# Product-key experts on one core: token innermost in the one-hots, bf16 operands in their comparisons and products

## What is computed

```python
q = (xf @ wq).reshape(T, 8, 2, 128)
s = jnp.einsum('thcd,ckd->thck', q, subkeys)
sv, si = lax.top_k(s, 16)                      # per head, per half
cand = (sv[:, :, 0, :, None] + sv[:, :, 1, None, :]).reshape(T, 8, 256)
cv, ci = lax.top_k(cand, 16)
ea = take_along_axis(si[:, :, 0], ci // 16);  eb = take_along_axis(si[:, :, 1], ci % 16)
experts = ea * 128 + eb                        # 128 experts for each token, of 16384
gate = softmax(cv)
act = gelu(einsum('cd,ced->ce', x, u_tab[experts]))
y = einsum('ce,ced->cd', act * gate, v_tab[experts])
```

## Time and profile before

| | |
|---|---|
| time, median of 3 runs | 4366.12 us (4361.21 to 4377.41) |
| the profiled execution's own time | 4377.61 us |
| its span | 4375.8 us |
| TensorE busy | 3942.4 us, 90% |
| VectorE busy | 2018.1 us, 46% |
| ScalarE, GpSimd busy | 895.2 us and 154.4 us |
| first layer's experts, first build to last chunk | 420.7 to 1262 us |
| second layer's experts, first build on | from 1670 us |

### The profile page before, as it was taken

The page is one execution under the profiler, slowest core; times in us unless marked ns, Lnnn a source line. Parts: engine busy times, 40 slices in busy tenths (PEclk is TensorE's granted clock), DMA queues, the critical chain, the costliest instruction groups (busy, mean ns, idle before and its releaser), DMA issues.

```text
span 4375.8 us, 54878 instructions
## 1 busy us (share of the span) xinstructions
PE 3942.4 (90%) x23468; PEld 2746.5 (63%) x23468; DVE 2018.1 (46%) x3441; ACT 895.2 (20%) x1502; POOL 154.4 (4%) x135
## 2 busy tenths in 40 slices
PE   6989999998988899999998979998869999999986
PEld 5778878886777688887876756565643333332333
DVE  4276645748754497255758533355532111111112
ACT  2311111223434111212233421223300000000000
POOL 0000000000000000000000000021200000000000
PEclk9799999999998899999999989999979999999998
DMA  4433323443344333333443331211129999999993
GB/s 182 155 135 138 132 116 131 159 155 135 135 165 155 134 137 125 124 136 135 154 154 123 137 127 49 106 58 58 58 81 413 427 428 427 428 427 428 425 398 145
DMA packets 62282, 846.18 MB, mean 193 GB/s; under 512 B 6800, under 2 KB 8976, under 8 KB 10160
## 3 DMA queue, kind: packets, MB, share of 16 engines
q1 hardware_dynamic: 62032, 842.60, 47.9%
HBM read 841.52 MB, written 1.05 MB: 193 GB/s over the span
## 4 chain that ended last, share of the span: by engine, by line
PE 67%; DVE 15%; DMA 13%; ACT 3%; issue 2%; SPq 0%; POOL 0%; DVEq 0%; ACTq 0%
PE bank L83 65%; DVE arena L119 6%; DMA ring<-in_w_gu_dram 6%; DMA ring<-in_peer_u_dram 3%; DMA arena<-in_w_gu_dram 3%; ACT arena L109 2%; DVE vlo L119 2%; PE bank L96 2%; DVE arena L187 1%; DVE arena L181 1%; DVE arena L193 1%; DVE arena L145 1%; DVE arena L133 1%; DVE arena L125 1%; DVE arena L127 1%
## 5 line engine op out<-in xcount | busy, mean ns | idle before, releaser
L83 PE MATMUL bank<-xT,ring 128*128 128x256 f32 x5120 | 1174.1, 389 | 55.7 <-DMA ring<-in_peer_u_dram 33.4
L83 PEld LDWEIGHTS bank<-xT,ring 128*128 128x128 f32 x5120 | 988.2, 195 | 197.8 <-DMA ring<-in_peer_u_dram 35.9
L83 PE MATMUL bank<-arena 128*128 128x32 bf16 (+7 forms) x9660 | 926.6, 291 | 145.7 <-DVE arena L119 108.5
L83 PEld LDWEIGHTS bank<-arena 128*128 128x128 bf16 (+4 forms) x9660 | 544.4, 126 | 522.9 <-issue 294.5
L83 PE MATMUL bank<-ring,arena 128*64 128x512 f32 (+1 forms) x2304 | 592.5, 606 | 39.5 <-DMA ring<-in_w_gu_dram 33.7
L109 ACT ACTIVATE arena<-bank 128x256 f32<-128x256 f32 (+2 forms) x484 | 223.8, 462 | 1975.2 <-PE bank L83 1484.6
L83 PEld LDWEIGHTS bank<-ring,arena 128*64 128x64 f32 (+1 forms) x2304 | 194.4, 146 | 427.3 <-issue 328.5
L119 DVE TENSOR_TENSOR arena<-arena 128x512 bf16<-128x512 bf16 (+6 forms) x636 | 424.4, 703 | 82.0 <-ACT arena L109 67.9
L119 DVE TENSOR_TENSOR vlo<-ring,vhi 128x1024 fp32r<-128x1024 f32 x256 | 313.2, 1224 | 267.2 <-PE bank L83 249.8
L83 PE MATMUL bank<-vhi,phi 128*128 128x512 f32 x1024 | 432.3, 422 | 0.0
L83 PE MATMUL bank<-vhi,plo 128*128 128x512 f32 x1024 | 406.7, 397 | 0.0
(11 more groups left out here) (105 smaller groups left out, 1665.9 us busy)
## 6 DMA issues: line engine op xcount, KB each, us to landing
ring<-in_w_gu_dram SPq DMA_DIRECT2D x85, 2048.0 KB, 19.3
ring<-in_peer_u_dram SPq DMA_DIRECT2D x64, 2048.0 KB, 8.7
ring<-in_peer_v_dram SPq DMA_DIRECT2D x64, 2048.0 KB, 8.6
arena<-in_w_gu_dram SPq DMA_DIRECT2D x55, 2048.0 KB, 19.4
ring<-in_w_dn_dram SPq DMA_DIRECT2D x41, 2048.0 KB, 17.9
arena<-in_w_dn_dram SPq DMA_DIRECT2D x29, 2048.0 KB, 20.6
ring<-in_w_hg_dram SPq DMA_DIRECT2D x14, 2048.0 KB, 8.6
ring<-in_w_mod_dram SPq DMA_DIRECT2D x12, 2048.0 KB, 7.8
```

The source lines that it names most:

```text
L83: i = self.e.matmul(o, l, r, start=start, stop=stop)
```

## The change

- `Aoh`, `Boh` and `eqb` keep their sizes, but the token becomes the innermost index: `(a t)` and `(b t)` in place of `(t a)` and `(t b)`.
- A new bf16 tensor `keys16` holds every key number repeated for 16 tokens (2048 values). GpSimd writes it at the start of each layer's experts and marks "keys listed"; VectorE waits for that mark ahead of the first hots.
- A new bf16 tensor `e16` holds a and b in bf16 (one conversion of 512 values a layer). The three gate parts are read from `gsb` in bf16, and the last part is written there directly.
- So the comparison and the products have three bf16 operands each, and the innermost index is the token, of step 1 in all of them. The value that is repeated is now repeated along the middle index.
- `pe_build` takes, for token i, the stationary operand `ah[:, :, i]` and the moving operand `bh[:, k, :, i]`: the 128 and the 32 columns now lie 16 elements (32 bytes) apart, where they were adjacent before.
- `eg` and `gs` move into the memory of the routing, which begins lower, and `ROUTED` becomes 45: five more chunks of stage 1 wait for "gates split".

```diff
-ROUTED = 50
+ROUTED = 45
...
+        e16 = ar(256).bitcast(BF16).rearrange("p (c n) -> p c n", c=2)
+        keys16 = ar(1024).bitcast(BF16).rearrange("p (a t) -> p a t", t=16)
...
-        Aoh = [ar(1024).bitcast(BF16).rearrange("p (t a) -> p t a", t=16) for _ in range(2)]
-        Boh = [ar(768).bitcast(BF16).rearrange("p (k t b) -> p k t b", k=3, t=16) for _ in range(2)]
-        eqb = [ar(256).bitcast(BF16).rearrange("p (t b) -> p t b", t=16) for _ in range(2)]
-        top[0] = ARENA - 11200
+        Aoh = [ar(1024).bitcast(BF16).rearrange("p (a t) -> p a t", t=16) for _ in range(2)]
+        Boh = [ar(768).bitcast(BF16).rearrange("p (k b t) -> p k b t", k=3, t=16) for _ in range(2)]
+        eqb = [ar(256).bitcast(BF16).rearrange("p (b t) -> p b t", t=16) for _ in range(2)]
+        top[0] = ARENA - 12736
...
             for i in range(16):
-                P.mm(bG[n % 2][:, i * 32:i * 32 + 32], [(ah[:, i, :], bh[:, k, i, :]) for k in range(3)])
+                P.mm(bG[n % 2][:, i * 32:i * 32 + 32], [(ah[:, :, i], bh[:, k, :, i]) for k in range(3)])
...
-            V.tt(Aoh[n % 2], bc(iota, 1, 16), bc(eg[:, 0, t0:t0 + 16], 2, 128), EQ, lag=FREE)
+            V.tt(Aoh[n % 2], keys16, bc(e16[:, 0, t0:t0 + 16], 1, 128), EQ, lag=0 if n < 2 else FREE)
...
-            V.tt(eqb[n % 2], bc(iota[:, q * 32:q * 32 + 32], 1, 16), bc(eg[:, 1, t0:t0 + 16], 2, 32), EQ, lag=FREE)
+            V.tt(eqb[n % 2], keys16[:, 32 * q:32 * q + 32, :], bc(e16[:, 1, t0:t0 + 16], 1, 32), EQ, lag=FREE)
...
-                V.tt(Boh[n % 2][:, k, :, :], eqb[n % 2], bc(gs[:, k, t0:t0 + 16], 2, 32), MUL, lag=k)
+                V.tt(Boh[n % 2][:, k, :, :], eqb[n % 2], bc(gsb[:, k, t0:t0 + 16], 1, 32), MUL, lag=k)
...
             V.cp(gsb[:, 0, :], eg[:, 2, :])
-            V.cp(gs[:, 0, :], gsb[:, 0, :])
+            V.cp(e16, eg[:, 0:2, :], lag=1)
+            V.cp(gs[:, 0, :], gsb[:, 0, :], lag=1)
...
-            V.tt(gs[:, 2, :], eg[:, 2, :], gs[:, 1, :], SUB)
+            V.tt(gsb[:, 2, :], eg[:, 2, :], gs[:, 1, :], SUB)
             V.mark("gates split", l)
+            V.wait_ge(*at["keys listed", l])
...
         def pool_peer(l):
             after_stage(G, "mix", l)
+            G.cp(keys16, bc(iota, 2, 16))
+            G.mark("keys listed", l)
```

More of the change, by code:

```diff
@@ L905, in build @@
         top[0] = 0
-        eg = ar4(3, 2, 128).rearrange("p k t n -> p k (t n)")
-        gs = ar4(3, 1, 256).rearrange("p k o n -> p k (o n)")
         gsb = ar(384).bitcast(BF16).rearrange("p (k n) -> p k n", k=3)
+        e16 = ar(256).bitcast(BF16).rearrange("p (c n) -> p c n", c=2)
+        keys16 = ar(1024).bitcast(BF16).rearrange("p (a t) -> p a t", t=16)
         H0 = top[0]
@@ L913, in build @@
         v_lo = [vlo_t[:, i * 1024:i * 1024 + 1024] for i in range(2)]
-        Aoh = [ar(1024).bitcast(BF16).rearrange("p (t a) -> p t a", t=16) for _ in range(2)]
-        Boh = [ar(768).bitcast(BF16).rearrange("p (k t b) -> p k t b", k=3, t=16) for _ in range(2)]
-        eqb = [ar(256).bitcast(BF16).rearrange("p (t b) -> p t b", t=16) for _ in range(2)]
-        top[0] = ARENA - 11200
+        Aoh = [ar(1024).bitcast(BF16).rearrange("p (a t) -> p a t", t=16) for _ in range(2)]
+        Boh = [ar(768).bitcast(BF16).rearrange("p (k b t) -> p k b t", k=3, t=16) for _ in range(2)]
+        eqb = [ar(256).bitcast(BF16).rearrange("p (b t) -> p b t", t=16) for _ in range(2)]
+        top[0] = ARENA - 12736
         assert H0 + 256 * ROUTED <= top[0]
+        eg = ar4(3, 2, 128).rearrange("p k t n -> p k (t n)")
+        gs = ar4(3, 1, 256).rearrange("p k o n -> p k (o n)")
         pq = [ar3(4, 256) for _ in range(2)]
```

## The result

The changed kernel takes 4592.19 us (median of 4 runs, 4588.51 to 4596.13) against 4368.38 us before: the ratio is 1.0511, 95% interval 1.0489 to 1.0533. That is 224 us more, where 38 to 40 were forecast. It lies inside the stated range and on the forecast side, but far outside the forecast's own range of 4385 to 4500.

A forecast was written before the change was run, and what follows sets the result against it. TensorE was taken as the bound, VectorE only in places. Per layer +13.1, +25.6 and −18.5 us made +20.2, so +40 for both layers on 4366: 4406 us; range 4258 to 4765, the forecast's own 4385 to 4500.

The forecast's parts named there:

- VectorE's rounds: VectorE's comparison and products per round: two bf16 values at a time, shortening a round by 2.12 us, from 5.33 to 3.21.
- stretch 3: Last window of a layer's experts, 165.3 us, 38 chunks of stage 2 and 16 builds; forecast 146.8 us, −18.5.
- The price of spread columns: TensorE's builds: a matmul with its load rises from 25 to 54 ns, a build by 1.39 us.
- a lost fast load: Rival, TensorE's builds: weight loads fall to float32 speed, 111 ns a matmul, +191 us a layer, 4747 us; chance 0.16.
- one column at a time: Rival, TensorE's builds: each of 128 stationary columns pays 1.68 ns in turn, 215 ns a matmul, 5382 us; chance 0.08.
- the free columns: Rival, TensorE's builds: spread columns cost nothing, 25 ns a matmul, −51 us a layer, 4264 us; chance 0.30.
- The clock: Last window of a layer's experts: 42.7 us lost to waits and lower clock come back, all but 2 us.
- stretch 1: First window of a layer's experts, 92.0 us, 16 builds and 18 chunks of stage 1; forecast 105.1 us, +13.1.
- stretch 2: Middle window of a layer's experts, 481.3 us, chunks 0 to 52, 32 builds, TensorE the bound; forecast +25.6 us.
- the loads of u: Middle window of a layer's experts: TensorE waits 16.0 us for these loads; 11 us given back by longer builds.
- the first rival: TensorE's builds: spread columns cost nothing, −51 us a layer, 4264 us in all; chance 0.30.
- The break-even point of 42 to 44 ns: TensorE's builds: time of one matmul with its load that decides between faster and slower, at 3.1 us a layer per ns.

## Why the prediction missed, step by step

**VectorE's rounds: right.** 1218 and 420 ns measured, 1225 and 421 taken, from rows with half the elements. TensorE's wait for hots went from 28.0 to 3.5 us in stretch 3; 2 were left over in the forecast.

**The price of spread columns: right in kind, too low.** This is the first of two terms that failed. The step "if TensorE pays 1.68 ns for each of the 32 moving columns, a matmul takes 54 ns" carried VectorE's price over. Alone they take 60 ns, 1.7 for each further one and a fixed rest, which the step left out. That 1.7 is VectorE's 1.68 again, of float32 values at twice the distance, no run explains; it may be chance. "128 columns need 49 ns, hidden behind the 54" was 62, and not quite hidden: both together take 67. The term was 1.39 us a build and measured 42·48 ns = 2.0 us. Over 128 builds that is 80 us more than forecast. The rivals of a lost fast load (111 ns) and of one column at a time (215 ns) didn't come; nor did the free columns.

**The clock: taken to come back whole, with no term for new falls.** This is the second, and the one where the mechanism was wrong, in the words "Stretch 3: 122.6 + 16·1.39 + 2 left over for waits". It took the 42.7 us lost there as VectorE's waits and the lower clock after them, and let all but 2 of it come back. That holds with TensorE's reading as it was (133.3 us at full clock). With the slower builds the clock fell all the same, now behind the builds themselves. Against the run with both operands adjacent, where only TensorE's reading differs:

| first layer | both adjacent | changed | more | builds, 2.0 us each | rest |
|---|---|---|---|---|---|
| stretch 1 | 88.1 | 119.3 | 31.2 | 32 | −1 |
| stretch 2 | 477.3 | 545.5 | 68.2 | 64 | +4 |
| stretch 3 | 133.3 | 187.9 | 54.6 | 32 | +23 |

In stretch 3 the rest is the clock's: 56 us at half speed are some 28 us lost. In stretch 2 the clock's mean is 0.95 where it was 0.97 with both adjacent, 55 us at half speed against some 29: about 13 us. Against them stand the loads of u, whose waits on TensorE went from 16.0 us to this:

```profile
PE bank L83 <- DMA ring<-in_peer_u_dram: 5.3, 2, 5.0
```

That is 10.7 us given back (both adjacent still has 15.7); the forecast had 11. In stretch 1, where stage 1 runs between the builds, the clock stays at 0.99.

**The sum.** Forecast for a layer: +13.1, +25.6, −18.5. Measured: +27.5, +63.9, +18.4, or 110 us in the first layer and 112 in the second (27.6, 62.8, 21.3). Of the 90 us too few in the first layer, 40 are the price of the columns (64·0.63 us). Some 7 are the saving on VectorE, 44 us in the three stretches where the first rival put 51 (82 us for the kernel, not 102). The 43 that are left stand in the table's last column: the forecast had −18 there (+20 for a layer is 71 above its free columns, and the builds were 89 of it) and +26 was measured, the clock above all. Either of the two alone would have brought the change to 120 us or more for both layers, three times the forecast. Between the two profiled executions the whole difference is 214 us, not 222: the second block, which the change doesn't touch, took 5 us less. The break-even point of 42 to 44 ns wasn't met by a run: 33 ns is 1.2% faster, 60 to 64 ns 4.9% slower, and a straight line between the two puts it near 39. The prediction's own figures give 42 ns counted up from the free columns (51 us at 3.1 us a ns) and 47 counted down from the forecast.

**The chances.** 0.58 for slower was right, and the forecast's own range left the clock out. A warning was in the rows: of the 42.7 us lost in stretch 3, TensorE stood still for 28.0 (165.30 − 137.31), and at a mean clock of 0.93 some 12 were matmuls at half speed. The rows did not show that an unbroken build could have the same effect; that took the runs.

## What to carry to other kernels

A layout serves two engines: look at both readers before turning an index innermost for one of them. Here VectorE needed only a run of two adjacent 16-bit values in every operand, and TensorE paid once its columns were 8 bytes apart or more, so blocks of two gave each what it needs. When small matmuls become slower one by one, look at the clock too: the wide matmuls behind them lost 23 us in stretch 3, on top of the builds' own 32.

## What of the hardware was not expected

- Spread columns cost TensorE the same in either operand, and the two prices overlap: 60 ns (32 moving), 62 ns (128 stationary), 67 ns (both), against 25 ns. The 128 stationary columns go four times as fast, one by one, as the moving ones.
- With four columns in 16 bytes such a matmul takes 25 ns, with two 33 ns, with one 60 to 64 ns.
- A build at 67 ns a matmul, without any pause in it, was followed by half clock each time in stretch 3; one with 25 ns and 32 columns never, at 2.4 us nor unbroken at 3.6 us.
- GpSimd repeats and converts 2048 values in 1.89 us, where its one float32 operation on two tensors had taken 6.5 us.
